# Taking the lower half of three weight units from an adding DMA instead of VectorE, in a two-block transformer kernel on one core

## The chip, the core and the metric

One core of one Trainium2 chip runs the whole program. The metric is the device time of one execution in microseconds (us). The engines are TensorE (PE; its weight loads are shown as PEld), VectorE (DVE), ScalarE (ACT), GpSimd (POOL) and SyncE (SP), which here only issues DMAs.

## What is computed

Two transformer blocks in a row over one sequence of 256 tokens and 1024 channels, all in float32:

```
x = first_block(x, ...)    # four attention branches, gates, MLP with relu squared, final norm
for l in range(DEPTH):     # second_block, DEPTH = 1
    h = rms_norm_2(x, norm1_g[l])
    proj = h @ w_in[l]                       # 1024 x 2560: the second input projection
    q, k, v, u = jnp.split(proj, [512, 1024, 1536], axis=-1)
    q = apply_rope(rms_norm_2(q, q_norm_g[l]), cos, sin)     # k likewise
    attn = moba_attention(q, k, v)           # 8 heads of 64
    conv = conformer_conv(u, ...)            # GLU, causal depthwise conv of 31 taps, LayerNorm, swish
    x = x + concat([attn, conv]) @ w_out[l]
    h = rms_norm_2(x, norm2_g[l])
    x = x + (silu(h @ w_gate[l]) * (h @ w_up[l])) @ w_down[l]
```

## The kernel before

Every large product is made from rounded halves. A weight unit is four blocks of 128 rows by 512 columns (128 partitions x 2048 elements, 1 MB). SP loads it into `raw`; ACT rounds it into `whi` (`split_hi`, L1167, the CAST rows); DVE subtracts to get the rest, `wlo = raw - whi` (`split_lo`, L1636). `product` (L668 to L670) then makes three matmuls for each row block and 512 columns: activation high x `whi`, high x `wlo`, low x `whi`. `raw`, `whi` and `wlo` have four slots each, so unit i uses slot i % 4. SP's `load(i)` (L560) waits until both halves of unit i - 4 are made; ACT's `split_hi(i)` waits until PE is done with unit i - 4.

The work of all engines is laid out by hand as a list of groups, one group for each `product` call. The second input projection has five chunks of 512 columns (`CH2`), each with two units (rows 0 to 511 and 512 to 1023), each used by two groups (token halves t = 0 and 1). That makes ten units and twenty groups. This text numbers them: unit (i, u) is half u of chunk i, and groups 0 to 19 run in the order (chunk, unit, t), so unit (2,0) is used by groups 8 and 9, unit (3,0) by 12 and 13, unit (4,0) by 16 and 17. ACT makes `whi` of unit (2,0) once group 1 is done, of (3,0) once group 5 is done, of (4,0) once group 9 is done; DVE makes `wlo` at the place of groups 3, 7 and 11.

Between these groups `timetable2` (`BG2`) places the rest of the block. PE turns parts of the projection (`ut` after groups 5, 6, 8, 9: L635; `rturn` after 14, 15, 18, 19). ACT makes the GLU's sigmoids (L1471), copies for the phases of the convolution (`ph`, L1483, L1484), drains PSUM (`evac2`, L1466) and squares q and k (`r0`, L1490). DVE finishes the GLU (`ug`, L2155, L2159), sums the squares (`r0`, L2109), makes the rotary products (`ra`, L2128 to L2135), scales (`r1`, L2142, L2147) and runs the taps of the convolution (`conv`, L2176, L2178). After group 19 come the attention heads: PE scores (`az`, L1016, L1017), DVE mask and minimum (`am`, L2192, L2194), ACT exponential (L1508, L1509).

POOL's program is short: reciprocal roots (`root`, L2323), which wait for a variance of DVE, and before the roots q0 to q3 four multiplications of the residual by the final gain (L2365), which start when the root r4 is done. SP's queue is in order, with `load(4,0)`, `load(4,1)`, the four units of the second output projection (`wo2`) and, ahead of the second of them, four small transfers to `hp` (L612, L613) that wait for `ph`.

Of the kernel before, what the change touches and what calls it, by code (L numbers as in the profile page):

```python
# [4 lines left out]
F32 = mybir.dt.float32  # L5
F32R = mybir.dt.float32r
ALU = mybir.AluOpType
# [8 lines left out]
NRAW = 4  # L16
NSPL = 4
# [166 lines left out]
def build(nc, ctx, x_d, xt_d, w_in, w_br, w_out, w_up, w_dn, w_in2, w_out2, w_g2, w_u2, w_gu, w_d2, par_d, par2_d, cst_d, tw_d, out_d):  # L184
    def sb(name, shape, dt=F32, c=ctx):
        return c.enter_context(nc.sbuf_tensor(name, shape, dt))
# [3 lines left out]
    raw = sb("raw", [128, NRAW, 2048])  # L190
    whi = sb("whi", [128, NSPL, 2048], F32R)
    wlo = sb("wlo", [128, NSPL, 2048], F32R)
# [58 lines left out]
    def sem(name):  # L251
        return ctx.enter_context(nc.semaphore(name))


    d_raw = [sem(f"d_raw{i}") for i in range(NRAW)]
    d_piece = [sem(f"d_piece{i}") for i in range(4 * NPC)]
    d_xt = [sem(f"d_xt{i}") for i in range(5)]
    d_cs0 = sem("d_cs0")
    d_x0, d_x1, d_par, d_cst, d_cs1, d_par2, d_tw, d_tw3, d_hp, d_out = [
# [9 lines left out]
    s_hi, s_xh, s_ev, s_sq = sem("s_whi"), sem("s_xhi"), sem("s_evac"), sem("s_squares")  # L269
# [7 lines left out]
    s_lo, s_xg, s_xl, s_var, s_lam = sem("s_wlo"), sem("s_xgain"), sem("s_xlo"), sem("s_var"), sem("s_lam")  # L277
# [14 lines left out]
    s_lg, s_sh, s_sd = sem("s_lg_round"), sem("s_sb_soft_hi"), sem("s_sb_soft_lo")  # L292
    s_g2 = sem("s_gfin_squared")
    s_warm = sem("s_warm")

    def pcol(name, i=0, n=1):
        o, w = PAR[name]
        return par[:, o + i:o + i + n]
# [19 lines left out]
    units = []  # L318
# [7 lines left out]
    unit_of = {}  # L326
# [61 lines left out]
    nu = len(units)  # L388
# [8 lines left out]
    for i in range(NPC, nu):  # L397
# [3 lines left out]
        g = max([g] + [h + 1 for h in split_after])  # L401
        split_after[g] = i
    HALF = [4 * (i + 1) if i < NPC else 4 * NPC + i - NPC + 1 for i in range(nu)]

    def landed(i):

        return d_raw[i % NRAW], 16 * (i // NRAW + (1 if i % NRAW >= NPC else 0))
# [133 lines left out]
    for key in X:  # L541
        k, a, n = key
# [8 lines left out]
    @block.sync  # L551
    def _(e):
        w = Gate(e)
        def load(i):
            v, kn, n = units[i]
            if i >= NRAW:
                w.wait_ge(s_hi, HALF[i - NRAW])
                w.wait_ge(s_lo, HALF[i - NRAW])
            dst = raw[:, i % NRAW, 0:kn * n].rearrange("p (k n) -> p k n", k=kn)
            e.dma_start(dst, v).then_inc(d_raw[i % NRAW], 16)  # L560

        def load_piece(i, k):
            v, kn, n = units[i]
            e.dma_start(raw[:, i, k * n:k * n + n], v[:, k, :]).then_inc(d_piece[4 * i + k], 16)

        def load_xt(i):
            a_, z_ = XP[i]
            e.dma_start(xT[:, a_:z_, :], xt_v[:, a_:z_, :]).then_inc(d_xt[i], 16)

        e.dma_start(raw[:, 0, 0:256], units[0][0][:, 0, 0:256]).then_inc(d_piece[0], 16)  # L570
        load_xt(0)
        load_xt(1)
        load_piece(0, 1)
        load_xt(2)
        load_piece(0, 2)
        load_piece(0, 3)
        load_xt(3)
        load_piece(1, 0)
        load_piece(1, 1)
        load_xt(4)  # L580
        load_piece(1, 2)
        load_piece(1, 3)
        for k in range(4):
            load_piece(2, k)
        e.dma_start(xr[:, 0, :], x_v[:, 0, :]).then_inc(d_x0, 16)
        e.dma_start(xr[:, 1, :], x_v[:, 1, :]).then_inc(d_x1, 16)
        for k in range(4):
            load_piece(3, k)
        e.dma_start(par[:], par_d).then_inc(d_par, 16)
        at = unit_of["up", 1, 0, 0]  # L590
        for i in range(NRAW, nu):
            if i == NRAW + 3:
                o = CST["MB"][0]
                e.dma_start(cs1[:, o:N1], cst_d[:, N0 + o:N0 + N1]).then_inc(d_cs0, 16)
            if i == NRAW + 4:
                e.dma_start(cst[:, 136:N0], cst_d[:, 136:N0]).then_inc(d_cs1, 16)
                e.dma_start(cs1[:, 0:CST["MB"][0]], cst_d[:, N0:N0 + CST["MB"][0]]).then_inc(d_cs1, 16)
            if i == at:
                w.wait_ge(s_mix, 4)
                w.wait_ge(s_pm, 8)  # L600
                w.wait_ge(s_xl, X["M", 1, 1] + 1)
                e.dma_start(par2[:], par2_d).then_inc(d_par2, 16)
            if i == unit_of["p2", 3, 0, 0]:

                w.wait_ge(s_mm, done("dn", 7, 1, 1))
                for q in range(3):
                    e.dma_start(tw[:, q, :], tw_d[:, 2048 * q:2048 * q + 2048]).then_inc(d_tw, 16)
            if i == unit_of["wo2", 0, 1, 0]:

                w.wait_ge(s_ph, 2)  # L610
                for k in range(2):
                    e.dma_start(hp[64:128, 2 * k, 0:143], odd[0:64, k, 0:143]).then_inc(d_hp, 16)  # L612
                    e.dma_start(hp[0:64, 2 * k + 1, 0:143], odd[64:128, k, 0:143]).then_inc(d_hp, 16)  # L613
            load(i)
        for k in range(4):
            t, n = k // 2, k % 2
            w.wait_ge(s_res, 12 + k + 1)
            e.dma_start(o_v[:, t, 512 * n:512 * n + 512], xr[:, t, 512 * n:512 * n + 512]).then_inc(d_out, 16)
        w.wait_ge(d_out, 64)
# [4 lines left out]
    def _(e):  # L624
        w = Gate(e)
# [20 lines left out]
        def product(tag, hi, lo, k0, t, bank_of, first, last, kr=None, at=None, cols=None, between=None):  # L646
            assert groups[tag] == count[0], (tag, count[0])
            count[0] += 1
            i = unit_of[tag]
            v, kn, n = units[i]  # L650
            H = whi[:, i % NSPL, 0:kn * n].rearrange("p (k n) -> p k n", k=kn)
            L = wlo[:, i % NSPL, 0:kn * n].rearrange("p (k n) -> p k n", k=kn)
            if i >= NPC:
                w.wait_ge(s_lo, HALF[i])
            krs = range(kn) if kr is None else kr
            for c0 in cols or (0,):
                ce = min(n, c0 + 512)
                for kc in krs:
                    if between and kc == 2:
                        between()  # L660
                    if at and kc in at:
                        w.wait_ge(*at[kc])
                    if i < NPC:
                        w.wait_ge(s_lo, HALF[i] - 3 + kc)
                    dst = bank_of(c0)[:, 0:ce - c0]
                    xh = hi[:, k0 + kc, t * 128:(t + 1) * 128]
                    xl = lo[:, k0 + kc, t * 128:(t + 1) * 128]
                    e.matmul(dst, xh, H[:, kc, c0:ce], start=first and kc == krs[0], stop=False)  # L668
                    e.matmul(dst, xh, L[:, kc, c0:ce], start=False, stop=False)  # L669
                    ins = e.matmul(dst, xl, H[:, kc, c0:ce], start=False, stop=last and kc == krs[-1])  # L670
            ins.then_inc(s_mm, 1)


        def first_chunk():

            count[0] = 4
            for k in range(8):
# [5 lines left out]
                w.wait_ge(s_xh, X["A", k, 0] + 1)  # L683
                w.wait_ge(s_hi, HALF[i] - 3 + kc)
                for t in range(2):
                    e.matmul(bank[3 + t], xh[t], H, start=k == 0, stop=False)
                w.wait_ge(s_xl, X["A", k, 0] + 1)
                for t in range(2):
                    e.matmul(bank[3 + t], xl[t], H, start=False, stop=False)
                w.wait_ge(s_lo, HALF[i] - 3 + kc)  # L690
                for t in range(2):
# [459 lines left out]
    def _(e):  # L1151
        w = Gate(e)
# [8 lines left out]
        def split_hi(i):  # L1161
            v, kn, n = units[i]
            s, r, m = i % NSPL, i % NRAW, kn * n
            w.wait_ge(*landed(i))
            if i >= NSPL:
                w.wait_ge(s_mm, free_at[i - NSPL])
            e.copy(whi[:, s, 0:m], raw[:, r, 0:m]).then_inc(s_hi, 1)  # L1167

        def piece_hi(i, k):

# [451 lines left out]
    def _(e):  # L1622
        w = Gate(e)
# [8 lines left out]
        def split_lo(i):  # L1632
            v, kn, n = units[i]
            s, r, m = i % NSPL, i % NRAW, kn * n
            w.wait_ge(s_hi, HALF[i])
            e.tensor_tensor(wlo[:, s, 0:m], raw[:, r, 0:m], whi[:, s, 0:m].bitcast(F32), ALU.subtract).then_inc(s_lo, 1)  # L1636
# [9 lines left out]
        def before(*tag):  # L1646

            i = split_after.get(groups[tag] - 1)
            if i is not None and i > split_done[0]:
                split_lo(i)  # L1650
                split_done[0] = i

        def x_lo(key, src=None):
# [38 lines left out]
        k = own(e.tensor_tensor(lscr, par[:, lo_:lo_ + 64], par[:, lo_ + 64:lo_ + 128], ALU.mult))  # L1692
# [622 lines left out]
    def _(e):  # L2315
        w = Gate(e)
# [4 lines left out]
        def root(key, r, v, n):  # L2321
            w.wait_ge(s_var, RS[key] + 1)
            e.tensor_tensor(r, v, mhalf[:, 0:n], ALU.pow).then_inc(s_rs, 1)  # L2323
# [39 lines left out]
        for t, n in ORD:  # L2363
            xs = xr[:, t, 512 * n:512 * n + 512]
            e.tensor_tensor(xs, xs, par2[:, 512 * n:512 * n + 512], ALU.mult).then_inc(s_pg, 1)  # L2365

        for i in range(4):
            root(f"q{i}", rpr[i], rpv[i], 8)
        for t in range(2):
            root(f"l{t}", lnr[t], lnv[t], 1)  # L2370
        root("r5", r5_, smx["r5"][1], 2)
# [101 lines left out]
```

## Time and profile before

| | us |
|---|---|
| Median of 3 runs | 770.51 (769.64 to 770.77) |
| Profiled execution, own time | 769.26 |
| Its span | 767.1 |
| DVE busy in the span | 586.2 |
| ACT busy in the span | 408.7 |
| POOL busy in the span | 53.2 |

The span is from the first to the last recorded instruction. The groups of the second input projection lie between 466 and 526 us in it, the attention heads and the convolution from there to 556 us. The rows further down are from the page of the profile and from views of its trace: times are the start in us from the start of the span and the length; what stands in brackets is the idle time of the engine before the instruction and what ended it. An instruction overlaps the one behind it on its engine by about 0.1 us, so a chain advances a little less than the lengths say.

### The profile page before, as it was taken

The numbers are of one execution on the slowest core, as the hardware profiler recorded it, in microseconds if no ns is written. First come the engines' busy times: TensorE is split into PE (matmuls) and PEld (weight loads), VectorE is DVE, ScalarE is ACT, GpSimd is POOL, SyncE is SP. The second block draws the span as 40 slices with busy tenths as digits, with TensorE's granted clock in tenths as the row PEclk, the third lists the DMA queues.
The fourth block names the chain that finished last, engine by engine and source line by source line (L and its number), as shares of the span: only waits on it lengthen the run. The fifth ranks groups of instructions, "written<-read, shape, count | busy, mean of one in ns | idle before, by whom it ended". The sixth has DMA issues, their size and how long they took to land.

```text
span 767.1 us, 9650 instructions
## 1 busy us (share of the span) xinstructions
PE 759.5 (99%) x3712; PEld 636.5 (83%) x3712; DVE 586.2 (76%) x956; ACT 408.7 (53%) x552; POOL 53.2 (7%) x42
## 2 busy tenths in 40 slices
PE   8999999999999999999999999999999999999998
PEld 6888899888888888888888888888988888888886
DVE  5879798687757877787778838799767777768584
ACT  6765455465647546556554545864665445353430
POOL 0200000000002400000000002541000000000000
PEclk9999999999999999999999999999999999999999
DMA  9953444354345567555565557654133766555601
GB/s 317 389 199 101 147 138 165 123 200 146 137 164 165 165 216 253 189 203 193 191 218 172 180 197 275 219 177 161 56 111 109 236 203 199 185 194 190 213 7 55
DMA packets 68796, 137.28 MB, mean 179 GB/s; under 512 B 2576, under 2 KB 6544, under 8 KB 68240
## 3 DMA queue, kind: packets, MB, share of 16 engines
q1 hardware_dynamic: 68320, 135.44, 52.0%
q10 hardware_dynamic: 432, 1.25, 0.5%
q8 instruction: 29, 0.48, 0.3%
q14 instruction: 15, 0.12, 0.0%
HBM read 135.48 MB, written 1.05 MB: 178 GB/s over the span
## 4 chain that ended last, share of the span: by engine, by line
PE 90%; DVE 6%; ACT 3%; issue 1%; DMA 1%; SPq 0%; ACTq 0%
PE b L668 20%; PE b L670 20%; PE b L669 19%; PE SS L668 4%; PE SS L670 4%; PE SS L669 4%; PE TT L635 3%; PE OO L668 2%; PE OO L670 2%; PE OO L669 2%; DVE wlo L1636 2%; DVE ca L2178 2%; PE b L835 1%; PE SS L782 1%; ACT whi L1167 1%; PE OO L1005 1%
## 5 line engine op out<-in xcount | busy, mean ns | idle before, releaser
L1636 DVE TENSOR_TENSOR wlo<-raw,whi 128x2048 fp32r<-128x2048 f32 (+2 forms) x119 | 270.4, 2273 | 78.8 <-ACT whi L1167 78.0
L1167 ACT CAST whi<-raw 128x2048 fp32r<-128x2048 f32 (+2 forms) x119 | 223.2, 1880 | 123.9 <-PE b L670 81.8
L668 PE MATMUL b<-whi,Ahi 128*128 128x512 f32 (+2 forms) x520 | 206.3, 397 | 0.1
L670 PE MATMUL b<-whi,Alo 128*128 128x512 f32 (+2 forms) x520 | 199.8, 384 | 0.0
L669 PE MATMUL b<-wlo,Ahi 128*128 128x512 f32 (+2 forms) x520 | 199.1, 383 | 0.0
L670 PEld LDWEIGHTS b<-whi,Alo 128*128 128x128 f32 x520 | 97.6, 188 | 19.9
L669 PEld LDWEIGHTS b<-wlo,Ahi 128*128 128x128 f32 x520 | 97.9, 188 | 17.9
L668 PEld LDWEIGHTS b<-whi,Ahi 128*128 128x128 f32 x520 | 97.8, 188 | 17.9 <-ACT gates L1242 0.3
L2037 DVE STREAM_TRANSPOSE hT<-ust 32x256 f32<-32x256 f32 (+1 forms) x192 | 81.5, 424 | 2.8
L668 PE MATMUL b<-whi,Bhi 128*128 128x512 f32 x154 | 60.4, 392 | 0.1
L670 PE MATMUL b<-whi,Blo 128*128 128x512 f32 x154 | 60.0, 389 | 0.0
L669 PE MATMUL b<-wlo,Bhi 128*128 128x512 f32 x154 | 60.0, 389 | 0.0
L670 PE MATMUL SS<-whi,hlo 128*128 128x512 f32 x108 | 42.0, 389 | 0.0
L668 PE MATMUL SS<-whi,hhi 128*128 128x512 f32 x108 | 42.0, 389 | 0.0
L669 PE MATMUL SS<-wlo,hhi 128*128 128x512 f32 x108 | 42.0, 389 | 0.0
L2323 POOL TENSOR_TENSOR st<-st 128x2 f32<-128x2 f32 (+3 forms) x13 | 20.2, 1560 | 264.2 <-DVE st L1669 264.2
L668 PEld LDWEIGHTS b<-whi,Bhi 128*128 128x128 f32 x154 | 28.9, 188 | 6.3 <-ACT ust L1410 0.5
L670 PEld LDWEIGHTS b<-whi,Blo 128*128 128x128 f32 x154 | 28.9, 188 | 6.1
L669 PEld LDWEIGHTS b<-wlo,Bhi 128*128 128x128 f32 x154 | 28.9, 188 | 5.9
L1290 ACT ACTIVATE Sb<-Sb,st 128x384 f32<-128x384 f32 (+3 forms) x16 | 9.9, 619 | 38.3 <-DVE st L1818 38.3
L1753 DVE STREAM_TRANSPOSE qkA<-gates 32x128 f32<-32x128 f32 x80 | 24.2, 302 | 1.3
L1188 ACT CAST hhi<-hT 128x512 fp32r<-128x512 f32 (+1 forms) x24 | 13.3, 603 | 20.8 <-DVE hT L2037 20.8
(306 smaller groups left out, 1104.3 us busy)
## 6 DMA issues: line engine op xcount, KB each, us to landing
raw<-in_w_in SPq DMA_DIRECT2D x38, 1024.0 KB, 5.0
raw<-in_w_up SPq DMA_DIRECT2D x16, 1024.0 KB, 5.4
raw<-in_w_dn SPq DMA_DIRECT2D x16, 1024.0 KB, 5.0
raw<-in_w_d SPq DMA_DIRECT2D x11, 1024.0 KB, 4.9
raw<-in_w_g SPq DMA_DIRECT2D x10, 1024.0 KB, 5.0
raw<-in_w_u SPq DMA_DIRECT2D x10, 1024.0 KB, 5.0
raw<-in_w_out SPq DMA_DIRECT2D x8, 1024.0 KB, 5.1
raw<-in_w_br SPq DMA_DIRECT2D x4, 1024.0 KB, 5.0
```

The costliest lines, as they stand in the source:

```text
L635: ins = e.transpose(dst[:, 128 * k:128 * k + 128], src[:, 128 * k:128 * k + 128], ident)
L668: e.matmul(dst, xh, H[:, kc, c0:ce], start=first and kc == krs[0], stop=False)
L669: e.matmul(dst, xh, L[:, kc, c0:ce], start=False, stop=False)
L670: ins = e.matmul(dst, xl, H[:, kc, c0:ce], start=False, stop=last and kc == krs[-1])
L1167: e.copy(whi[:, s, 0:m], raw[:, r, 0:m]).then_inc(s_hi, 1)
L1188: e.copy(ph, src).then_inc(s_xh, 1)
L1290: ins = e.activation(P, P, ACT.Exp, bias=stat_m[i][:, 0:1], accum_out=stat_s[i][:, 0:1])
L1636: e.tensor_tensor(wlo[:, s, 0:m], raw[:, r, 0:m], whi[:, s, 0:m].bitcast(F32), ALU.subtract).then_inc(s_lo, 1)
L1753: ins = e.transpose(tile[:, :, :, 32 * k:32 * k + 32], src[32 * k:32 * k + 32, :, :, 32 * m:32 * m + 32])
L2037: ins = e.transpose(dst[32 * m:32 * m + 32, :, :, 32 * i:32 * i + 32], src[32 * i:32 * i + 32, :, :, 32 * m:32 * m + 32])
L2178: k_tap[k] = own(e.scalar_tensor_tensor(out=ca[:, k, :], in0=x, scalar=tap, in1=ca[:, k, :], op0=ALU.mult, op1=ALU.add))
L2323: e.tensor_tensor(r, v, mhalf[:, 0:n], ALU.pow).then_inc(s_rs, 1)
```

## The change

For units (2,0), (3,0) and (4,0) DVE no longer subtracts. ACT, directly after rounding, waits for its own rounding and writes the negated rounded half into the `wlo` slot; POOL then issues a DMA that adds `raw` onto it, so that `wlo = -whi + raw`. Those who waited for `s_lo` of these units wait for the DMA's semaphore (`lo_done`): PE ahead of the first product with the unit, and SP ahead of the load into the same `raw` slot. POOL issues the first two DMAs after the four multiplications and the third behind root q0.

```diff
+    d_rest = [sem(f"d_rest{i}") for i in range(3)]
...
+    RD = [unit_of[tag] for tag in (('p2', 2, 0, 0), ('p2', 3, 0, 0), ('p2', 4, 0, 0))]
+    LOWS = [HALF[i] - sum(j <= i for j in RD) for i in range(nu)]
+    def lo_done(i):
+        return (d_rest[RD.index(i)], 16) if i in RD else (s_lo, LOWS[i])
...
 # SP, load(i)
-                w.wait_ge(s_lo, HALF[i - NRAW])
+                w.wait_ge(*lo_done(i - NRAW))
 # PE, product
-                w.wait_ge(s_lo, HALF[i])
+                w.wait_ge(*lo_done(i))
 # ACT, split_hi
             e.copy(whi[:, s, 0:m], raw[:, r, 0:m]).then_inc(s_hi, 1)
+            if i in RD:
+                w.wait_ge(s_hi, HALF[i])
+                e.mul(wlo[:, s, 0:m], whi[:, s, 0:m].bitcast(F32), -1.0).then_inc(s_neg, 1)
 # DVE, before
-                split_lo(i)
+                if i not in RD:
+                    split_lo(i)
 # POOL, after the multiplications by par2
+        def rest(k):
+            s, r, m = RD[k] % NSPL, RD[k] % NRAW, units[RD[k]][1] * units[RD[k]][2]
+            w.wait_ge(s_neg, k + 1)
+            e.dma_start(wlo[:, s, 0:m], raw[:, r, 0:m], accum_op=ALU.add).then_inc(d_rest[k], 16)
+        for k in range(len(RD) - 1):
+            rest(k)
         for i in range(4):
             root(f"q{i}", rpr[i], rpv[i], 8)
+            if i == 0:
+                rest(len(RD) - 1)
```

## Rows read from the trace of the kernel before

**Rows 1.** Page, part 1: busy time, share of the span, instructions

```profile
PE 759.5 (99%) x3712; PEld 636.5 (83%) x3712; DVE 586.2 (76%) x956; ACT 408.7 (53%) x552; POOL 53.2 (7%) x42
```

**Rows 2.** Chain that ended last, 492 to 530 us: start, length, what

```profile
492.63 0.45 PE TT L635 x4
493.37 0.35 DVE ch L2155
...
501.33 2.28 DVE wlo L1636
...
529.21 0.40 DVE S L2194
```

**Rows 3.** PE in order of time, from 489 us

```profile
489.74 0.39 PE L668 MATMUL b<-whi,Ahi 128*128 128x512 f32 x1
...
513.28 0.48 PE L668 MATMUL b<-whi,Ahi 128*128 128x512 f32 x1
...
522.80 0.66 PE L635 MATMUL TT<-cst,PT 128*128 128x128 f32 x4 [1.08 <-DVE PT L2147]
...
527.66 0.60 PE L1017 MATMUL SS<-qk2T 128*128 128x256 f32 x2
```

**Rows 4.** DVE in order of time, 479 to 529 us

```profile
479.91 2.28 DVE L1636 TENSOR_TENSOR wlo<-raw,whi 128x2048 fp32r<-128x2048 f32 x1
483.18 5.62 DVE L1636 TENSOR_TENSOR wlo<-raw,whi 128x2048 fp32r<-128x2048 f32 x2 [0.99 <-ACT whi L1167]
493.11 0.61 DVE L2155 SCALAR_TENSOR_TENSOR ch<-TT,par,ca 128x128 f32<-128x128 f32 x2 [4.31 <-PE TT L635]
...
500.53 0.68 DVE L2109 TENSOR_REDUCE st<-tg 128x8 f32<-128x512 f32 x1
...
505.54 0.68 DVE L2109 TENSOR_REDUCE st<-tg 128x8 f32<-128x512 f32 x1
...
528.85 0.35 DVE L2192 CUSTOM_DVE_ANT_0 S<-SS,cst,st 128x128 f32<-128x128 f32 x1
```

**Rows 5.** ACT in order of time, 480 to 505 us

```profile
480.08 1.27 ACT L1466 ACTIVATE ys<-b,st 128x512 f32<-128x512 f32 x2 [5.18 <-DVE st L2105]
...
483.61 1.92 ACT L1167 CAST whi<-raw 128x2048 fp32r<-128x2048 f32 x1 [0.47 <-PE OO L670]
...
494.27 0.51 ACT L1483 COPY hp<-tg 64x64 f32<-64x64 f32 x2 [1.84 <-DVE tg L2159]
...
495.91 1.91 ACT L1167 CAST whi<-raw 128x2048 fp32r<-128x2048 f32 x1 [0.20 <-PE b L670]
...
499.78 0.64 ACT L1490 ACTIVATE tg<-ust 128x512 f32<-128x512 f32 x1
501.77 0.69 ACT L1466 ACTIVATE ust<-b,st 128x512 f32<-128x512 f32 x1 [1.35 <-PE b L670]
...
504.16 0.63 ACT L1490 ACTIVATE tg<-ust 128x512 f32<-128x512 f32 x1
```

**Rows 6.** POOL: L2365 (ns min/median/max), then two roots in time

```profile
L2365 POOL TENSOR_TENSOR xr<-xr,par x4: 1287/3340/3419, 478.7 to 486.6; 128x512 f32<-128x512 f32 x4
...
501.50 3.61 POOL L2323 TENSOR_TENSOR st<-st 128x8 f32<-128x8 f32 x1 [11.56 <-DVE st L1669]
506.50 2.01 POOL L2323 TENSOR_TENSOR st<-st 128x8 f32<-128x8 f32 x1 [1.39 <-DVE st L1669]
```

**Rows 7.** SP: the issue of one load; all loads from 440 to 560 us

```profile
482.26 0.37 SPq L560 DMA_DIRECT2D raw<-in_w_in  x1
...
DMA to landing us min/median/max: 4.9/5.0/8.6
```

**Rows 8.** Windows: PE, PEld, DVE, ACT, POOL busy, PEclk, DMA share, GB/s

```profile
466.00:478.00 12.00, 12.00 (x59) 9.93 (x58) 11.17 (x22) 7.67 (x9) 2.96 (x2) 1.00 1.02 413
...
766.00:767.00 1.00, 0.00 (x0) 0.00 (x0) 0.00 (x0) 0.00 (x0) 0.00 (x0) 0.67 0.24 88
```

**Rows 9.** PE in order of time, its first and its last instructions

```profile
1.31 2.93 PE L699 MATMUL OO<-Blo 128*128 128x512 f32 x6 [1.31 <-POOL Blo L2317]
...
763.57 0.39 PE L670 MATMUL b<-whi,hlo 128*128 128x512 f32 x1
```

More of the change, by code:

```diff
@@ L294, in build @@
     s_warm = sem("s_warm")
+    s_neg = sem("s_whi_negated")
     def pcol(name, i=0, n=1):
```

## The prediction

> **What bounds the kernel now.** I read the page first, then the chain that ended last, then each engine's instructions in order of time around the three units. PE is busy for 99% of the span, DVE for 76% [rows 1]. So relieving DVE can pay only where PE waits for it. In the second input projection the chain is DVE from 493.4 to 529.6, with no gap: the subtraction of unit (4,0) at 501.33, 2.28 us, stands in it [rows 2]. But PE waits in that stretch just once, 1.08 us at 522.80, for the rotary product scaled by L2147 [rows 3]. The two engines are nearly level there.
>
> **What each of the three subtractions is worth.** DVE subtracts (2,0) at 479.91 and (3,0) as the second of the two that start at 483.18; both lie ahead of a DVE idle stretch of 4.31 us that ends only when PE's turn after group 8 arrives, at 493.11 [rows 4]. Removing them moves nothing on the chain: worth 0. Removing (4,0)'s takes 2.2 us (2.28 less the overlap) out of the chain. How far could 2.2 reach? PE could run 1.08 us earlier from 522.80 on; the first scores, whose last matmuls start at 527.66 and are in by 528.1, would be in by 527.0. DVE takes them at 528.85 [rows 3, 4]. So this stretch can be shortened by at most 528.85 - 527.0 = 1.8 us, even if the rest of the change were free.
>
> **What ACT's three negations cost.** The trace of before has no such instruction; the nearest is the CAST of the same 128x2048, 1.91 us, and behind it the next instruction starts after 1.8 [rows 5]. The negation has to wait for the cast's own end, so I count 1.9. Lower bound is the cast's 1.8, upper bound the two of them one after the other, 3.8, for which nothing speaks. For (2,0) it falls into the 5.18 us that ACT idles before 480.08: 0. For (3,0) it goes behind the cast at 483.61 and pushes the sigmoids and the cast of the next unit; the work between there and 494.27 has 1.84 us of idle at its end, which swallows it: 0. For (4,0) it goes behind the cast at 495.91, and behind it in ACT's order are the second set of phase copies, the evacuation and the square of q at 499.78, which ended at 500.42. DVE's sum of that square starts at 500.53 [rows 4, 5], 0.1 us later. The negation is therefore on the chain: the sum moves to 502.4, DVE idles 1.9, and then saves 2.2, a net -0.3. Next in line is the second square: ACT had 1.35 us of idle before 501.77, now none, so the square of 504.16 moves to about 504.8 and its sum, 505.54 before, starts at about 505.4. So what is left of the 2.2 us is -0.1. The gain has been moved from DVE to ACT, and ACT spends it on the same chain.
>
> **When POOL can issue the first adding DMA.** It stands behind four multiplications (L2365) and these start at 478.68, right after root r4. Alone one takes 1.29 us, but three of the four took 3.3 to 3.4 [rows 6]: each of these ran beside a subtraction of DVE. Of the three subtractions beside them, (2,0)'s is now gone, which lets the second, third and fourth run before (2,1)'s begins at 483.18 or just into it. So POOL is done at 478.68 + 4 x 1.25 = 483.7, not at 489.9. The negation is long finished, (2,0) being rounded by 475 and negated by 477.
>
> **What the adding DMA takes, X, from POOL's issue to PE's release.** Nothing in the trace adds in a DMA. A load of the same 1 MB lands 5.0 us after issue (4.9 to 8.6) [rows 7]; that is the lower bound, since an add moves at least as much. An add must also read its destination: one more MB. In the densest window the DMAs moved 413 GB/s [rows 8], so a further MB costs 2.5 us. For the issue on POOL I add 0.6 (between the 0.37 us that an issue on SP lasts [rows 7] and the 1.29 us of a multiplication on POOL; an estimate). X = 5.0 + 2.5 + 0.6 = 8.1. Upper bound: if adding ran at a third of that rate, 2 MB in and 1 out as separate passes and slower by half, 2.5 + 3 x 2.5 x 1.5 = 14. I take 8.1, since the loads' row is the nearest in size and shape.
>
> The Trainium skill bears on this, in "Collectives: The Full Stack", Stop ④ and "Why ReduceScatter is half of AllGather": an add in the DMA path costs no time for the adding but a second source read, so about twice a copy's reading. No run here shows it yet. With the fixed 2.0 us and 436 GB/s of "DMA: Bandwidth & Descriptors" (two cost components) that would be 2.0 + 4.8 = 6.8 us instead of 8.1, an estimate from those pages, and the sum below would come out 1.3 lower, at the edge of what can be told from no change.
>
> **Sum.** Unit (2,0) is needed by group 8, at 489.74 [rows 3]. It is there at 483.7 + 8.1 = 491.8: PE stalls 2.1 us. During that stall DVE and ACT have nothing else to do, since all they have left waits for PE's turn after group 8; so the stall passes through whole. +2.1.
> SP is blocked at `load(4,0)` until then, where before it issued at 482.3 [rows 7]. The load starts at 491.8, has the rest of the second adding DMA (issued at 487.4, when (3,0) is negated) beside it, and lands at some 499; ACT would round (4,0) at 495.91 + 2.1 = 498.0. I count half of the 1 us between as real: +0.5, directly on the ACT and DVE chain above. `load(4,1)` is behind it and lands by about 502, just in time.
> The second adding DMA, for (3,0), has from 487.4 to group 12 at 503.7: hidden, up to X = 16.
> The third: root q0 starts with the sum at about 503.3 and takes 2.0 (it took 3.61 at 501.50 beside the subtraction now gone, the next one 2.01 [rows 6]), so issue at 505.3; 8.1 plus 1.3 for the load of the output projection that now falls beside it: 514.7. Group 16 wants it at 513.28 [rows 3]. 1.4 late (all of these shift together with the first stall), covered by the 1.08 that PE waits at 522.80 and the 0.75 from 528.1 to 528.85: 0. Root q1 waits behind this issue on POOL; its taker is DVE at 511.4, 5 us after its variance, and there is room for it.
> Together 2.1 - 0.1 + 0.5 = +2.5 us. On the profiled execution's 769.26 this gives 771.8; the median of the runs is 770.51, 1.25 higher, so 773.0. After this stage nothing makes up for it: heads, convolution and output projection all hang on the same chain.
>
> 0.2% (1.5 us) is about what a measurement of this kernel can tell from no change.
>
> **Rivals.**
> *The adding DMA is quick (X up to 7.1).* The stall is 1.1 or less, with the other terms +1.5 or less: 770.4 to 772.0, no measurable change. For it: DMA queues nearly empty at that time. Against: only the plain load's 5.0. Chance 0.26.
> *It is slow, as X = 12.* Stall 12 - 6.0 = 6.0. Then PE's clock may fall too: at the end PE's last matmul starts at 763.57 and the granted clock averages 0.67 in the stretch from 766 [rows 8, 9], so it fell to the lower of 1.2 and 2.4 GHz within some 2.5 us of idleness. At the start six matmuls took 2.93 us [rows 9], where they take 6 x 0.23 at full clock: +1.5. The third DMA is then 12 + 1.3 - 8.0 = 5.3 late, 1.8 covered: +3.5. With the +0.4 of the small terms: 11.4, so 782. Chance 0.25, over X from 9.6 up.
> *POOL isn't released.* If its multiplications still end at 489.9, or writing descriptors is held up by DVE's subtraction of (2,1) and what follows, the issue comes up to 6.2 late: stall 8.2, clock 1.5, small terms 0.4: 10, so 780.5. It decides against my sum as soon as the multiplications after (2,0) still last 3.3. Chance 0.08.
> *Faster.* One mechanism: ACT's negation of (4,0) does not hold up the square of q (it is much shorter than a cast, or the phase copies have slack that I don't see), and X stays below 6.0. Then the bound of 1.8 above counts: 768.7. The 0.1 us between square and sum speaks against it. Chance 0.06.
> My forecast, X from 7.1 to 9.6, is +1.5 to +4.3: 772.0 to 774.8, chance 0.35.
>
> **How the numbers follow.** Slower by over 0.2%: 0.35 + 0.25 + 0.08 = 0.68; within: 0.26; faster: 0.06. The range reaches from 770.0, where X hits its lower bound, to 783, which holds X up to about 12.5 with the clock's fall; outside are the gain and the slowest adds. The likeliest case's own range is 772.0 to 774.8.
>
> **What the profile after would show.** A PE wait before the first matmul of group 8 that ends with the DMA: right if 1 to 3.5 us; if there is none, X is below 6.0. All four L2365 near 1.3 us. Three ACT instructions of about 1.9 us behind the casts. The sum at L2109 with about 1.9 us of DVE idle before it, released by ACT's square. DMA transfers of 1 MB from POOL's queue with some 8 us to landing. The PE wait at L635 for L2147 smaller or gone, perhaps one at group 16. I am wrong in the main if X is far from 8, if PE's clock falls at the first stall, or if SP's late load of (4,0) holds ACT up by more than a microsecond.

## The result and the profile after

| | before | after |
|---|---|---|
| Median of 5 runs, us | 770.51 | 774.86 (773.89 to 775.18) |
| Ratio of the runs | | 1.0056, 95% interval 1.0042 to 1.0070 |
| Profiled execution, own time, us | 769.26 | 774.86 |
| Span, us | 767.1 | 772.9 |

Slower by 0.56%, 4.35 us between the medians (3.2 to 5.4 by the interval). The forecast was 773.0, slower, with 770.0 to 783.0 as the range and 772.0 to 774.8 for the likeliest case. The sign held, and the size was nearly twice what the sum gave (+2.5); it lies just outside the likeliest case. The two profiled executions differ by more, 5.6 us, since the one of before (769.26) is 1.25 below its median.

Line numbers have moved: L668 to L670 are now L677 to L679, L635 is L644, L1636 is L1648, L1167 is L1176, L2109 is L2122, L2147 is L2160, L2192 is L2205, L2323 is L2336, L2365 is L2378, L1466 is L1478, L1490 is L1502, L560 is L569. New are L1179, the negation, and L2383, the adding DMA. All of this trace stands some 0.5 us later than before's already at the start of the stage, so 0.5 has to be taken off before times are compared.

The page after: busy time as in [rows 1], and the new queue.

```profile
PE 761.9 (99%) x3712; PEld 638.8 (83%) x3712; DVE 579.0 (75%) x953; ACT 413.5 (53%) x555; POOL 48.1 (6%) x45
...
q0 software_dynamic: 432, 3.15, 2.1%
```

DVE is busy 7.2 us less and POOL 5.1 less, ACT 4.8 more; the time is longer all the same. POOL in order of time, the answer to [rows 6]:

```profile
479.19 5.04 POOL L2378 TENSOR_TENSOR xr<-xr,par 128x512 f32<-128x512 f32 x4
484.19 1.02 POOL L2383 DMA_DIRECT2D wlo<-raw  x1
488.30 0.87 POOL L2383 DMA_DIRECT2D wlo<-raw  x1 [3.10 <-ACT wlo L1179]
507.82 2.04 POOL L2336 TENSOR_TENSOR st<-st 128x8 f32<-128x8 f32 x1 [18.64 <-DVE st L1682]
509.82 0.90 POOL L2383 DMA_DIRECT2D wlo<-raw  x1
```

The four multiplications take 5.04 us instead of 11.3, as each is free of the subtraction beside it. The first issue is at 484.19. Now the chain that ended last, in order of time (start, length, what):

```profile
484.19 7.12 DMA wlo<-raw
...
491.37 8.98 DMA raw<-in_w_in
...
500.38 1.92 ACT whi L1176
...
502.33 1.92 ACT wlo L1179
...
506.84 0.70 DVE st L2122
...
507.82 2.00 POOL st L2336
509.82 9.34 DMA wlo<-raw
...
519.30 0.47 PE b L677
```

Where DVE's work was an unbroken chain [rows 2], the chain is now three DMAs with short instructions between them: the first add, behind it SP's load of unit (4,0), behind that ACT's rounding and negation, the square, its sum on DVE, root q0 on POOL, and then the third add, which POOL could issue only behind that root. PE in order of time, as [rows 3]:

```profile
491.36 0.50 PE L677 MATMUL b<-whi,Ahi 128*128 128x512 f32 x1 [0.93 <-DMA wlo<-raw]
...
519.30 0.47 PE L677 MATMUL b<-whi,Ahi 128*128 128x512 f32 x1 [3.98 <-DMA wlo<-raw]
...
521.34 0.63 PE L678 MATMUL b<-wlo,Ahi 128*128 128x512 f32 x1
```

Group 8 starts at 491.36 where before, moved by 0.5, would be at 490.25: 1.1 late. Group 16 starts at 519.30 instead of 513.8: 5.5 late, after 4 us of idling. The first matmuls behind it still take 0.39, and from 520.52 on they take 0.60 to 0.63. The windows show why (columns as in [rows 8]):

```profile
517.00:519.00 2.00, 0.00 (x0) 0.00 (x0) 1.97 (x4) 2.00 (x3) 0.76 (x1) 1.00 0.21 41
519.00:521.00 2.00, 1.70 (x7) 1.43 (x8) 2.00 (x3) 0.57 (x2) 2.00 (x1) 0.88 0.40 20
521.00:523.00 2.00, 2.00 (x6) 1.56 (x5) 1.93 (x5) 0.00 (x0) 0.85 (x1) 0.50 0.83 306
```

The granted clock is 1.00 while PE idles, begins to fall after PE has resumed, and is 0.50 (1.2 instead of 2.4 GHz) from 521 to 523. DVE in order of time, as [rows 4]:

```profile
494.89 0.61 DVE L2168 SCALAR_TENSOR_TENSOR ch<-TT,par,ca 128x128 f32<-128x128 f32 x2 [8.51 <-PE TT L644]
...
506.84 0.69 DVE L2122 TENSOR_REDUCE st<-tg 128x8 f32<-128x512 f32 x1 [4.43 <-ACT tg L1502]
...
509.74 0.69 DVE L2122 TENSOR_REDUCE st<-tg 128x8 f32<-128x512 f32 x1
...
534.61 0.35 DVE L2205 CUSTOM_DVE_ANT_0 S<-SS,cst,st 128x128 f32<-128x128 f32 x1 [1.47 <-PE SS L1026]
```

DVE idles 4.43 us ahead of the first sum of squares and 1.47 ahead of the first scores. And ACT, as [rows 5]:

```profile
486.08 1.92 ACT L1179 ACTIVATE wlo<-whi 128x2048 fp32r<-128x2048 f32 x1
...
500.38 1.91 ACT L1176 CAST whi<-raw 128x2048 fp32r<-128x2048 f32 x1 [2.88 <-DMA raw<-in_w_in]
502.33 1.92 ACT L1179 ACTIVATE wlo<-whi 128x2048 fp32r<-128x2048 f32 x1
```

The reader can now add up. A measure that all kernels here share is the stretch from DVE's subtraction of unit (1,1) (475.87 before) to its first work on the scores (528.85 before): 52.98 us. After it is 534.61 - 476.38 = 58.23, +5.25. Behind it nothing differs: from there to the first product of the output projection both take 28.0. The 5.25 are 1.1 (first add late) + 2.9 (ACT waits for the load) + 1.9 (negation) - 2.2 (subtraction gone), 3.7, and 1.5 in which DVE waits for a PE that is late by its stall at group 16 and by the clock. How much of this 1.5 is the third add's own doing is a question for third_back below.

### The profile page after: what moved, and what is told of

Same layout as the page of the kernel before. It is cut to its first block, busy times and chain, and to the rows that moved or that the text cites. A ratio compares the mean times of both kernels' runs of the same rounds, so it can differ in the third digit from the quotient of the medians.

```text
span 772.9 us, 9653 instructions
## 1 busy us (share of the span) xinstructions
PE 761.9 (99%) x3712; PEld 638.8 (83%) x3712; DVE 579.0 (75%) x953; ACT 413.5 (53%) x555; POOL 48.1 (6%) x45
## 3 DMA queue, kind: packets, MB, share of 16 engines
q10 hardware_dynamic: 432, 1.25, 0.5%
## 4 chain that ended last, share of the span: by engine, by line
PE 84%; DVE 5%; DMA 4%; ACT 3%; POOL 1%; issue 1%; ACTq 0%; POOLq 0%; SPq 0%
PE b L677 19%; PE b L679 19%; PE b L678 19%; PE SS L677 4%; PE SS L679 4%; PE SS L678 4%; DMA wlo<-raw 2%; PE TT L644 2%; PE OO L677 2%; PE OO L679 2%; PE OO L678 2%; DVE wlo L1648 1%; DMA raw<-in_w_in 1%; DVE ca L2191 1%; PE b L844 1%
## 5 line engine op out<-in xcount | busy, mean ns | idle before, releaser
L1648 DVE TENSOR_TENSOR wlo<-raw,whi 128x2048 fp32r<-128x2048 f32 (+2 forms) x116 | 262.9, 2268 | 81.1 <-ACT whi L1176 80.4
L1176 ACT CAST whi<-raw 128x2048 fp32r<-128x2048 f32 (+2 forms) x119 | 222.9, 1878 | 130.1 <-PE b L679 87.5
L677 PE MATMUL b<-whi,Ahi 128*128 128x512 f32 (+2 forms) x520 | 207.1, 398 | 5.0 <-DMA wlo<-raw 4.9
L679 PE MATMUL b<-whi,Alo 128*128 128x512 f32 (+2 forms) x520 | 200.5, 386 | 0.0
L677 PEld LDWEIGHTS b<-whi,Ahi 128*128 128x128 f32 x520 | 98.2, 189 | 23.4 <-issue 4.2
L679 PEld LDWEIGHTS b<-whi,Alo 128*128 128x128 f32 x520 | 97.9, 188 | 20.0
L677 PE MATMUL b<-whi,Bhi 128*128 128x512 f32 x154 | 60.4, 392 | 0.1
L679 PE MATMUL b<-whi,Blo 128*128 128x512 f32 x154 | 60.0, 389 | 0.0
L679 PE MATMUL SS<-whi,hlo 128*128 128x512 f32 x108 | 42.0, 389 | 0.0
L677 PE MATMUL SS<-whi,hhi 128*128 128x512 f32 x108 | 42.0, 389 | 0.0
L2336 POOL TENSOR_TENSOR st<-st 128x2 f32<-128x2 f32 (+3 forms) x13 | 18.7, 1440 | 271.1 <-DVE st L1682 271.1
L677 PEld LDWEIGHTS b<-whi,Bhi 128*128 128x128 f32 x154 | 28.9, 188 | 6.4 <-ACT ust L1422 0.5
L679 PEld LDWEIGHTS b<-whi,Blo 128*128 128x128 f32 x154 | 28.9, 188 | 6.0
```

## The experiments

The stretch is the one just named, in the profiled execution of each; "DVE waits" is what stands in brackets at its end. Each ratio is taken to executions of the kernel before that were measured along with that kernel (their medians lie between 769.99 and 770.51). plain_copy has one execution and no interval.

| Kernel | Median, us | Ratio to before (95%) | Stretch, against 52.98 | DVE waits |
|---|---|---|---|---|
| changed kernel | 774.86 | 1.0056 (1.0042 to 1.0070) | +5.25 | 1.47 |
| third_back | 773.92 | 1.0049 (1.0037 to 1.0061) | +4.95 | 0.96 |
| root_behind | 774.39 | 1.0051 (1.0039 to 1.0063) | +4.78 | 0.93 |
| first_early | 774.36 | 1.0047 (1.0034 to 1.0060) | +5.44 | 2.78 |
| first_only | 772.07 | 1.0029 (1.0017 to 1.0041) | +1.61 | - |
| third_only | 770.00 | 0.9999 (0.9990 to 1.0007) | -0.07 | - |
| skip_first | 769.66 | 0.9995 (0.9986 to 1.0004) | -0.05 | - |
| negate_only | 773.11 | 1.0038 (1.0023 to 1.0053) | +2.88 | 0.93 |
| negate_busy | 772.19 | 1.0029 (1.0018 to 1.0041) | +1.86 | - |
| no_lows | 770.01 | 1.0002 (0.9993 to 1.0010) | -0.07 | - |
| before_taps | 771.98 | 1.0020 (1.0010 to 1.0030) | +1.60 | - |
| third_taps | 768.94 | 0.9987 (0.9978 to 0.9995) | -0.07 | - |
| plain_copy | 770.86 | - | +0.61 | - |

**Which of the three adding DMAs costs.** Theory A: the first, through SP's queue. Theory B: the third.

third_back, from the changed kernel (both DMAs ahead of the roots, none behind root q0):

```diff
-    RD = [unit_of[tag] for tag in (('p2', 2, 0, 0), ('p2', 3, 0, 0), ('p2', 4, 0, 0))]
+    RD = [unit_of[tag] for tag in (('p2', 2, 0, 0), ('p2', 3, 0, 0),)]
...
-        for k in range(len(RD) - 1):
-            rest(k)
+        rest(0)
+        rest(1)
         for i in range(4):
             root(f"q{i}", rpr[i], rpv[i], 8)
-            if i == 0:
-                rest(len(RD) - 1)
```

> Only (2,0) and (3,0) by the adding DMA, (4,0) back on VectorE. Theory A, the late first DMA (a stall of PE of 1.1 us ahead of group 8, then the load of (4,0) that SP issues only behind it and that lands 2.9 us too late for ScalarE's cast): nothing pays for these 4.0 us, and there is no stall at group 16 any more, so the first sum of squares is about 4.0 us later than before and the median is 774.0 to 774.7, hardly better than the changed kernel. Theory B, the third DMA with PE's stall of 4.0 us and its clock's fall is what costs: the first stall is only 1.1 us, so 771.6.

It came out as A has it: 773.92, 0.1 below the expected 774.0 to 774.7, and 4.95 less the final wait of 0.96 is the 4.0 that was expected. Theory B's 771.6 is outside the interval. The final wait of 0.96 says something more. PE does not stall at group 16 here; it idles later instead, at the turn that waits for DVE's L2160:

```profile
526.69 1.11 PE L644 MATMUL TT<-cst,PT 128*128 128x128 f32 x4 [3.72 <-DVE PT L2160]
```

Behind this stretch the granted clock is 0.50 too (from 528 to 530). So a late DVE chain alone brings PE's idling and the fall of the clock. The third add makes the stretch only 0.3 longer than it is without it (5.25 against 4.95).

third_only:

```diff
-    RD = [unit_of[tag] for tag in (('p2', 2, 0, 0), ('p2', 3, 0, 0), ('p2', 4, 0, 0))]
+    RD = [unit_of[tag] for tag in (('p2', 4, 0, 0),)]
...
-        for k in range(len(RD) - 1):
-            rest(k)
         for i in range(4):
             root(f"q{i}", rpr[i], rpv[i], 8)
             if i == 0:
-                rest(len(RD) - 1)
+                rest(0)
```

> Only (4,0) by the adding DMA, behind root q0. Theory A: the load of (4,0) is not late, ScalarE's negation costs 1.9 and VectorE's missing subtraction gives 2.2 back, root q0 ends near 505.3, the DMA lands 9 us later at about 514.5, up to 1.3 us late for group 16 and covered by PE's wait behind it: 770.0 to 771.5, no change. Theory B, the third DMA is the cost by itself: 773 or more, with a PE stall of 4 us at group 16.

No change, 0.9999. PE's wait for the DMA in it, in order of time:

```profile
514.43 0.47 PE L677 MATMUL b<-whi,Ahi 128*128 128x512 f32 x1 [1.20 <-DMA wlo<-raw]
```

So late as that it is covered by PE's later wait, as the prediction's sum had it for a third add that comes on time. Its DMA took 9.3 us here too, with a load beside it that SP had issued at 503.37.

skip_first gives the adding DMA to (3,0) and (4,0) and leaves (2,0) to DVE:

```diff
-    RD = [unit_of[tag] for tag in (('p2', 2, 0, 0), ('p2', 3, 0, 0), ('p2', 4, 0, 0))]
+    RD = [unit_of[tag] for tag in (('p2', 3, 0, 0), ('p2', 4, 0, 0),)]
...
-        for k in range(len(RD) - 1):
-            rest(k)
+        rest(0)
         for i in range(4):
             root(f"q{i}", rpr[i], rpv[i], 8)
             if i == 0:
-                rest(len(RD) - 1)
+                rest(1)
```

> Units (3,0) and (4,0) by the adding DMA, (2,0) back on VectorE. Theory: the whole loss comes from the first unit, whose DMA can't be ready for group 8 and holds SP's loads back until a second adding DMA lies beside them. Without it the load of (4,0) is issued at 482 as before, the DMA for (3,0) has from about 488 to 501.6, and that for (4,0) is 1.2 us late under PE's later wait: 770.0 to 771.0, ratio within 0.2% of 1. Rival: two adding DMAs cost through SP's queue (the first load of the output projection waits for (3,0)) or through contention, wherever they stand: 772 or more.

0.9995: two of the three units cost nothing. The loss hangs on unit (2,0).

first_only keeps that unit alone:

```diff
-    RD = [unit_of[tag] for tag in (('p2', 2, 0, 0), ('p2', 3, 0, 0), ('p2', 4, 0, 0))]
+    RD = [unit_of[tag] for tag in (('p2', 2, 0, 0),)]
...
-        for k in range(len(RD) - 1):
-            rest(k)
+        rest(0)
         for i in range(4):
             root(f"q{i}", rpr[i], rpv[i], 8)
-            if i == 0:
-                rest(len(RD) - 1)
```

> Only (2,0) by the adding DMA. PE stalls 1.1 us at group 8 as in the changed kernel; the load of (4,0) is again issued at 491.4 but no second adding DMA lies beside it. If that DMA was what made the load take 9.0 us, it lands in 5.0 to 5.5 at 496.6, ahead of the cast, and the total is +1.1: 771.6. If the load is slow for another reason (two loads issued together), it lands near 500 and the total is +4: 774.5.

The ratio is 1.0029, the stretch +1.61 (the add took 7.5 here and PE waited 1.31). What it was made for is ACT's rounding of (4,0), in order of time:

```profile
497.47 1.91 ACT L1176 CAST whi<-raw 128x2048 fp32r<-128x2048 f32 x1 [0.20 <-PE b L679]
```

It waits for PE, no longer for the load, which landed 5.2 us after its issue. So the load of 9.0 us in the changed kernel was slow because a second transfer from POOL lay beside it; the two together, not the first alone, cost 4. Whether that second transfer had to be an adding one is seen in plain_copy below.

**Two orders on POOL.** root_behind issues the third add ahead of root q0:

```diff
-        for k in range(len(RD) - 1):
-            rest(k)
+        rest(0)
+        rest(1)
+        rest(2)
         for i in range(4):
             root(f"q{i}", rpr[i], rpv[i], 8)
-            if i == 0:
-                rest(len(RD) - 1)
```

> The changed kernel with the third adding DMA issued ahead of root q0 instead of behind it. It waits then for ScalarE's negation alone (504.2), is issued 5 us earlier and lands at about 513.5, ahead of group 16. Theory A: the stall of 4.0 us and the fall of the clock are gone, the 3.7 us of the chain of VectorE and ScalarE stay, so about 1.5 us less than the changed kernel: 773.2 to 773.8. Theory B: all of the 4.3 us go, 770.5 to 771.5.

The stall at group 16 went, as expected, but the time hardly did: 774.39 for 773.2 to 773.8. The expectation had left out that PE, no longer stalled at group 16, comes to the turn that waits for DVE's L2160 the earlier, and DVE is 3.8 us late. Its windows:

```profile
522.00:524.00 2.00, 0.62 (x3) 0.19 (x1) 1.93 (x6) 0.00 (x0) 1.47 (x1) 1.00 1.03 401
524.00:526.00 2.00, 0.00 (x0) 0.00 (x0) 2.00 (x5) 0.00 (x0) 0.55 (x1) 1.00 0.06 23
526.00:528.00 2.00, 1.70 (x9) 1.45 (x10) 2.00 (x2) 1.00 (x2) 0.00 (x0) 0.86 0.00 0
528.00:530.00 2.00, 2.00 (x6) 1.59 (x5) 2.00 (x5) 0.17 (x1) 0.00 (x0) 0.50 0.24 27
```

PE idles 3.7 us there and the clock falls all the same. The idle time had only moved.

first_early puts the first add ahead of the four multiplications:

```diff
         root("r4", smx["r4"][2], smx["r4"][1], 2)
...
+        rest(0)
         w.wait_ge(s_sq, SQ["N2", 1, 1] + 1)
...
-        for k in range(len(RD) - 1):
-            rest(k)
+        rest(1)
         for i in range(4):
             root(f"q{i}", rpr[i], rpv[i], 8)
             if i == 0:
-                rest(len(RD) - 1)
+                rest(2)
```

> The changed kernel with the first adding DMA issued ahead of GpSimd's four multiplications, 5 us earlier. Theory A: it lands at about 487, no stall at group 8, SP issues the load of (4,0) at 487 and it lands by 495.9; the sum of squares is later by the negation's 1.9 only, which the missing subtraction pays; the third DMA is issued at about 506 and is hidden but for 1 us: 770.3 to 771.8, no measurable change from before. Theory B: the stall at group 16 stays, 773 or more.

This failed, at 774.36 (one of its six executions took 771.73, at a mean granted clock of 0.999; the others had 0.996 or 0.997 and took 773.91 to 775.31). The chain that ended last in first_early:

```profile
479.48 11.73 DMA wlo<-raw
...
491.27 8.26 DMA raw<-in_w_in
```

Issued 4.7 us earlier, the add landed at the same time, after 11.7 us instead of 7.1. SP's load of (3,1) was issued just ahead of it (479.04) and the DMA engines were full from 482 to 488. One more MB at the 393 GB/s that a full window shows is 2.7 us (an estimate), so the load beside it accounts for some 2.7 of the 4.6. From 480 to 490 the DMAs moved 2.1 MB, as much as the load and the add together, and from 489 to 490 the engines were almost idle (share 0.13). Why the add still landed only at 491.2 stays open.

**What ACT's negations cost.** negate_only adds them to the kernel before and lets DVE wait for them and then subtract as ever:

```diff
             e.copy(whi[:, s, 0:m], raw[:, r, 0:m]).then_inc(s_hi, 1)
+            if i in RD:
+                w.wait_ge(s_hi, HALF[i])
+                e.mul(wlo[:, s, 0:m], whi[:, s, 0:m].bitcast(F32), -1.0).then_inc(s_neg, 1)
...
             w.wait_ge(s_hi, HALF[i])
+            if i in RD:
+                w.wait_ge(s_neg, RD.index(i) + 1)
             e.tensor_tensor(wlo[:, s, 0:m], raw[:, r, 0:m], whi[:, s, 0:m].bitcast(F32), ALU.subtract).then_inc(s_lo, 1)
```

> The kernel before with ScalarE's three negations added; VectorE waits for them and subtracts as before, so the result is unchanged and only ScalarE's work is more. Theory: the first two are in idle time of ScalarE, the third moves the square of q, so VectorE's first sum by 1.9 us and the end with it: 772.2 to 772.6. Rival: the phase copies and the evacuation have slack, no change.

773.11, more than the 1.9 us. DVE of this kernel in order of time:

```profile
503.78 0.69 DVE L2117 TENSOR_REDUCE st<-tg 128x8 f32<-128x512 f32 x1 [1.77 <-ACT tg L1496]
...
533.12 0.35 DVE L2200 CUSTOM_DVE_ANT_0 S<-SS,cst,st 128x128 f32<-128x128 f32 x1 [0.93 <-PE SS L1020]
```

And its windows around that last wait:

```profile
524.00:526.00 2.00, 0.00 (x0) 0.00 (x0) 2.00 (x6) 0.00 (x0) 0.30 (x1) 1.00 0.00 1
526.00:528.00 2.00, 1.95 (x7) 1.76 (x8) 2.00 (x1) 0.80 (x2) 0.00 (x0) 0.50 0.00 0
```

1.9 of the 2.88 are the negation of (4,0) on the chain, as predicted. 0.93 is a PE at half clock after a wait of 2.9 us. To show that it is the clock, negate_busy fills the wait:

```diff
                 elif name == "r2":
+                    if i == 2:
+                        clear(3)
+                        for _ in range(10):
+                            e.matmul(bank[3], Ahi[:, 0, 0:128], Ahi[:, 0:2, :], start=True, stop=True)
                     rturn(i)
```

> The run with the negations alone, with ten matmuls of 512 columns into a PSUM bank that nobody reads put ahead of the turn for which PE idled 2.9 us; the output is unchanged. Theory: of the 2.8 us that the negations alone cost, 1.9 is VectorE's chain and 0.9 is PE's clock, which was at 0.50 from 526 to 528. With PE busy the granted clock stays at 1.00, VectorE's wait of 0.93 us for the first scores goes, and the ratio falls from 1.0038 to about 1.0026. Rival: the 0.9 us is PE's own work behind the late turn, which stays whatever the clock is: 1.0038 or more.

The same window in negate_busy:

```profile
526.00:528.00 2.00, 1.89 (x11) 1.64 (x12) 2.00 (x2) 1.18 (x2) 0.00 (x0) 1.00 0.00 0
```

The clock stays, DVE's wait is gone, the stretch is +1.86. The intervals of the ratios (1.0029 and 1.0038) overlap and would not tell the two apart by themselves; the traces do. The mean granted clock of each execution points the same way: in negate_only four of six had 0.998 or less and took 772.69 to 774.19 us, two had 1.000 and took 770.96 and 771.22. In negate_busy all six had 1.000 and took 771.62 to 772.62. (Why those two are a little faster than these six stays open.)

**The most that the change could give.** no_lows leaves out the three subtractions, and with them the waits for them, so that PE multiplies with what the slot held and part of the projection's precision is missing (the edits of the waits are not shown):

```diff
-                split_lo(i)
+                if i not in RD:
+                    split_lo(i)
```

> The kernel before with the three subtractions left out and nothing in their place: PE multiplies with what the slot held, so part of the projection's precision is missing from the output. It measures the most that the change could give. The prediction's bound says up to 1.8 us (768.7). The theory after reading the trace: VectorE's next sums wait for ScalarE's squares (504.8 instead of 505.5) and then for PE's group 14 (512.96 instead of 513.06), so the 2.2 us are gone again after two groups: 770.0 to 770.6.

1.0002. DVE in order of time:

```profile
505.39 0.69 DVE L2113 TENSOR_REDUCE st<-tg 128x8 f32<-128x512 f32 x1 [1.40 <-ACT tg L1493]
...
513.56 0.69 DVE L2113 TENSOR_REDUCE st<-tg 128x8 f32<-128x512 f32 x1 [0.56 <-ACT tg L1493]
```

The 2.2 us are idle time again at the next sums (1.40 and 0.56 us), and the stretch is only 0.07 shorter. There was nothing to win in this place.

**What adding costs in a DMA.** plain_copy lets the three DMAs of the changed kernel copy `raw` onto the slot, so that the lower halves of three units are wrong:

```diff
-            e.dma_start(wlo[:, s, 0:m], raw[:, r, 0:m], accum_op=ALU.add).then_inc(d_rest[k], 16)
+            e.dma_start(wlo[:, s, 0:m], raw[:, r, 0:m]).then_inc(d_rest[k], 16)
```

> The changed kernel with the three DMAs copying raw onto the slot instead of adding, so the lower halves of three units are wrong in the output. It measures what adding costs. If the second read sets the add's time, the first DMA lands 2 to 2.5 us sooner (about 4.9 instead of 7.1), if the issue and the receipt set it, it takes the same 7.1.

The first copy landed in 4.87 us, the first add in 7.12. A window of the copy in plain_copy, with no other transfer beside it:

```profile
487.00:488.00 1.00, 1.00 (x8) 0.79 (x7) 0.06 (x1) 1.00 (x1) 0.00 (x0) 1.00 1.03 393
```

And the window of the add in first_only, where no other transfer lies beside it:

```profile
485.00:490.00 5.00, 4.85 (x24) 3.68 (x22) 3.02 (x2) 4.63 (x12) 0.00 (x0) 1.00 1.03 210
```

The DMA engines are full in both, and the add moves about half: 210 for 393 GB/s.

plain_copy also serves as a control for the whole loss, since it differs from the changed kernel in nothing but the adding. PE does not wait at group 8, and the stretch is +0.61 instead of +5.25. So 4.6 of the 5.25 hang on the slower adding (one trace of each). But the load of (4,0) is slow here too, in order of time in the chain:

```profile
489.79 8.16 DMA raw<-in_w_in
```

It takes 8.2 us beside a second plain copy, 9.0 beside a second add, 5.2 beside neither (first_only). So most of its delay comes from any second transfer of 1 MB that lies beside it, and only 0.8 from its being an add. What the adding did above all is to hold the load's issue back, behind a first DMA that came 2.25 us later: ACT waited 1.07 us for the load here, 2.88 in the changed kernel. plain_copy's 770.86 us is a single execution.

**A version that beats both.** The negation leaves DVE 1.75 us idle ahead of its first sum. Among the attention heads DVE is on the chain. third_taps moves four taps of the convolution from there into that gap, on top of third_only; before_taps makes the same move in the kernel before, as a control:

```diff
-    for s, n in ((10, 8), (12, 2), ...
+    for s, n in ((10, 12), (12, 2), ...
...
-            conv(6 if k < 4 else 4 if k < 8 else 1)
+            conv(5 if k < 4 else 4 if k < 8 else 1)
```

> Only (4,0) by the adding DMA, and four of the convolution's taps moved from among the attention heads into VectorE's idle stretch of 1.75 us ahead of its first sum of squares. Theory: the idle time that ScalarE's negation leaves takes them for nothing, and the heads, where VectorE is on the chain, end 1 to 1.6 us sooner: 768.6 to 769.3, ratio 0.998 to 0.9987. Rival: among the heads ScalarE and PE are the chain as much as VectorE, no change.

> The kernel before with the same four taps moved, as a control: here VectorE has no idle time for them. Theory: its chain up to the first scores is 1.6 us longer, PE idles 2.7 us and its clock may fall, the heads give 1.6 back: ratio 1.000 to 1.001. Rival: moving the taps is what gains, with or without the DMA: 0.998.

third_taps: 768.94, ratio 0.9987, clear of no change, if by little, and its interval overlaps that of third_only. The idle time is used, as DVE in order of time shows in third_taps:

```profile
503.07 0.69 DVE L2122 TENSOR_REDUCE st<-tg 128x8 f32<-128x512 f32 x1 [0.17 <-ACT tg L1502]
```

The stretch is as long as before, and from its end to the output projection it is 27.1 instead of 28.0 us. The control gains the same 0.9 there and pays 1.60 for it ahead, +0.7 in the profiled execution (770.63 us). Its ratio of 1.0020 is more than that, and its executions fall into two groups: five at a mean granted clock of 1.000 took 769.95 to 770.63, six at 0.998 or 0.995 took 771.98 to 773.28. So the fall that its expectation feared came in six of eleven; the profiled one is not among them. Even the five at full clock are no faster than before. So the gain is neither the DMA's nor the move's alone: the DMA takes 2.2 us of DVE's work away, the move uses them.

## Why the prediction was right, and where it was off

The sign and the order of the size were right, and part of that was luck. With the X that was measured, 7.17 us from POOL's issue to PE's release, the prediction's own sum gives 483.7 + 7.2 - 489.74 = 1.1 for the stall and +1.5 in all, the upper end of what it calls no measurable change. The kernel was slower by 4.35 because two other terms came out larger. Of its signs of being wrong in the main, one came true: SP's late load held ACT up by more than a microsecond (2.88). Its test for the first stall, a wait of 1 to 3.5 us, was missed by little (0.93).

**POOL's release.** The prediction had the multiplications end at 483.7; less the 0.5 us, they ended at 483.7. Right, and with it the rival in which POOL isn't released falls.

**The add, X = 8.1.** 7.12 for the first. The term for the second read was 2.5 us, plain_copy gives 2.25; the term for the issue, 0.6, was too much, since a copy from POOL took 4.87, no longer than a load from SP [rows 7]. The first stall was thus 1.1 instead of 2.1. Beside a load the third took 9.3 us, which the sum had right, as 8.1 plus 1.3 for the load. The estimate of 6.8 us from the Trainium skill's pages ("Collectives: The Full Stack", "Why ReduceScatter is half of AllGather", for the second source read, and the two cost components of "DMA: Bandwidth & Descriptors" for the 2.0 us and 436 GB/s) is nearer to the 7.12 than my 8.1. On the second source read the trace agrees: at full DMA engines the add moves about half of what the copy moves, 210 for 393 GB/s.

**SP's late load.** This is the step that failed in size: "I count half of the 1 us between as real: +0.5". The load took 9.0 us, not 7.2, with the second add beside it, and ACT waited 2.9 us. first_only shows that the neighbour is the cause: without the second add the load takes 5.2 and ACT does not wait for it at all. plain_copy shows that a plain copy as the neighbour does most of this too (8.2). Three things add up to the miss, all with the 0.5 us taken off: the load landed at 499.8 where the prediction had 499; ACT was free for it at 497.0, not 498.0, because the first stall was shorter; and the halving ("half of the 1 us") had no row behind it. The stall and this term together were forecast at 2.6 and came to 4.0.

**ACT's negation.** Length (1.92), the first two absorbed, the third on the chain: right, negate_only. That it cancels against the subtraction: right, third_only.

**The third add.** "1.4 late ..., covered: 0" holds for an add that comes on time (third_only, 1.2). But it hangs on root q0, that on the sum, and the sum on the late load, while PE's groups were late by 1.1 only. "All of these shift together" was wrong: it was then 4.4 us behind PE, 4.0 of stall. Together with the clock it is 1.5 beyond DVE's own lateness; but third_back, without a third add, has 0.96 of that wait as well, from the late load. So the third add's net cost is 0.3, and the term that was missing is PE's idling behind a late DVE. I had the fall of the clock only in the rival for X = 12; it came with X at 7 to 9.

**The sum.** Predicted 2.1 + 0.5 - 0.1 + 0 = 2.5; found 1.1 + 2.9 - 0.3 + 1.5 = 5.2 in the two traces, 4.35 in the medians. One more slip stands in the likeliest case: at its end, X = 9.6, the sum's own terms give 3.6 + 0.4 + 1.1 (the third DMA 2.9 late, 1.8 covered) = +5.1, not +4.3, so that it should have ended at 775.6.

**The bound of the gain.** "At most 1.8 us" was too loose: no_lows gives 0.0. I had followed DVE's chain to the end of the stage and not looked at who releases each of its steps once it runs 2.2 us ahead. The prediction had done so for the first two sums; the third, released by PE's group 14 through ACT at 512.96, was 0.1 us away.

## What to carry to other kernels

Before work is taken off an engine, walk its chain with the work gone and ask at each step who releases it next: 2.2 us that stood in the middle of an unbroken chain were worth nothing. A transfer put in the place of an instruction brings its latency to every queue that waits for it: here the same DMA cost nothing for units with 8 and 14 us of room (third_only, skip_first), and 1.6 us for one that had 6 (first_only), or 4 and more when a second one lay beside the next load in SP's order (third_back). Where one engine frees time, something must be moved into it, or it is only idle.

## What was not expected of the hardware

An adding DMA within SBUF moved 210 GB/s where a copy of the same shape moved 393, with the DMA engines full in both cases. A load of 1 MB took 9.0 us beside an add and 8.2 beside a copy from POOL, instead of 5.0. PE's granted clock was seen at 0.50 after idle stretches of 2.9, 3.3 (first_early), 3.7 and 4.0 us, and stayed 1.00 after one of 2.7 in the profiled execution of before_taps. Such a fall cost up to 1 us of the stretch (negate_only against negate_busy). The same program can meet it in one execution and not in the next: before_taps had a mean clock below 1.000 in six of eleven, with a median of 772.5 us against 770.4 for the others. Those six have no trace, so the place of the fall is not shown for them. An add that was issued 4.7 us earlier beside a load took 11.7 us and came no earlier, and part of that is unexplained.
